# HGRN2 recurrence in four pairs of heads, its level updates on VectorE between the projections of the next pair

## The reference

```
q, z_fw, z_bw, i, g = split(h @ w_in, 5)          # each 512 x 1024, 8 heads of 128
log_f = log(lb + (1 - lb) * sigmoid(z));  k = 1 - exp(log_f)      # per direction
S_t = diag(f_t) S_{t-1} + k_t outer v_t ;  o_t = S_t^T silu(q_t)  # per head and direction
o = rmsnorm(o_fw + o_bw, out_norm) * silu(g);  return o @ w_o
```

## Time and profile before

| | us |
|---|---|
| median of 3 runs (lowest, highest) | 2341.68 (2337.03, 2342.49) |
| the profiled execution's own time | 2341.26 |
| its span, first to last instruction | 2339.5 |
| TensorE busy, share of the span | 2114.2, 90% |
| VectorE, ScalarE, GpSimd busy | 936.7, 614.8, 841.7 |
| mean granted clock | 0.939 |

### The profile page before, as it was taken

How to read it: one execution, slowest core, us unless ns; L and a number is a source line. 1 busy time by engine, 2 the same in 40 slices (tenths; PEclk the granted TensorE clock), 3 DMA queues, 4 the chain that set the end, 5 groups by cost and what they waited for, 6 DMA issues and landing times.

```text
span 2339.5 us, 31254 instructions
## 1 busy us (share of the span) xinstructions
PE 2114.2 (90%) x12424; PEld 1711.4 (73%) x12424; DVE 936.7 (40%) x1186; ACT 614.8 (26%) x789; POOL 841.7 (36%) x360
## 2 busy tenths in 40 slices
PE   7999999888999999999999977965997489999997
PEld 5888887644778888878888866754875477788885
DVE  4434414555273331145343123175318535543212
ACT  4222223233242222233222233210231023222221
POOL 2444442200224444424444442362246212444442
PEclk9999999899999999999999998976997589999998
DMA  3223332200223223322233321210121012332332
GB/s 137 95 94 99 92 97 80 63 18 1 74 71 99 90 98 92 99 79 91 98 98 92 93 85 54 85 44 1 55 82 48 1 37 80 91 99 90 94 99 76
DMA packets 51640, 179.68 MB, mean 77 GB/s; under 512 B 5728, under 2 KB 5856, under 8 KB 51552
## 3 DMA queue, kind: packets, MB, share of 16 engines
q1 hardware_dynamic: 51552, 178.40, 23.9%
HBM read 176.28 MB, written 2.10 MB: 76 GB/s over the span
## 4 chain that ended last, share of the span: by engine, by line
PE 73%; issue 13%; DVE 6%; POOL 6%; ACT 2%; DMA 1%; SPq 0%; POOLq 0%; DVEq 0%; ACTq 0%
PE psum L481 23%; PE psum L482 22%; PE psum L483 22%; POOL w_lo L403 3%; POOL k_lev L423 2%; PE psum L700 1%; DVE att L1263 1%; DVE prob L1275 1%; PE psum L693 1%; DVE q_lev L1334 0%; PE psum L761 0%; PE psum L573 0%; DVE xt L1101 0%; PE psum L819 0%; DVE t_a L1096 0%
## 5 line engine op out<-in xcount | busy, mean ns | idle before, releaser
L403 POOL TENSOR_TENSOR w_lo<-raw,w_hi 128x1024 fp32r<-128x1024 f32 (+1 forms) x324 | 766.5, 2366 | 1399.6 <-ACT w_hi L885 1399.6
L481 PE MATMUL psum<-xg_hi,w_hi 128*128 128x512 f32 x1832 | 730.7, 399 | 38.8 <-DMA const<-consts 15.8
L482 PE MATMUL psum<-xg_lo,w_hi 128*128 128x512 f32 x1832 | 722.5, 394 | 0.0
L483 PE MATMUL psum<-xg_hi,w_lo 128*128 128x512 f32 x1832 | 722.3, 394 | 0.0
L885 ACT ACTIVATE w_hi<-raw 128x1024 fp32r<-128x1024 f32 (+1 forms) x339 | 352.1, 1039 | 1046.3 <-DMA raw<-w_up 492.0
L481 PEld LDWEIGHTS psum<-xg_hi,w_hi 128*128 128x128 f32 x1832 | 348.7, 190 | 117.6 <-DMA const<-consts 15.8
L483 PEld LDWEIGHTS psum<-xg_hi,w_lo 128*128 128x128 f32 x1832 | 347.8, 190 | 80.1
L482 PEld LDWEIGHTS psum<-xg_lo,w_hi 128*128 128x128 f32 x1832 | 348.6, 190 | 74.7 <-issue 0.2
L481 PE MATMUL psum<-hid_hi,w_hi 128*128 128x512 f32 x704 | 273.9, 389 | 0.0
L483 PE MATMUL psum<-hid_hi,w_lo 128*128 128x512 f32 x704 | 273.9, 389 | 0.0
L482 PE MATMUL psum<-hid_lo,w_hi 128*128 128x512 f32 x704 | 273.9, 389 | 0.0
(11 more groups left out here) (162 smaller groups left out, 1499.2 us busy)
## 6 DMA issues: line engine op xcount, KB each, us to landing
raw<-w_up SPq DMA_DIRECT2D x176, 512.0 KB, 3.5
raw<-w_down SPq DMA_DIRECT2D x64, 512.0 KB, 3.6
raw<-w_hgrn SPq DMA_DIRECT2D x48, 512.0 KB, 3.5
raw<-w_down SPq DMA_DIRECT2D x32, 384.0 KB, 3.1
raw<-w_mla SPq DMA_DIRECT2D x19, 512.0 KB, 3.5
xt<-x_t SPq DMA_DIRECT2D x8, 256.0 KB, 6.4
out<-xt SPq DMA_DIRECT2D x8, 256.0 KB, 2.0
const<-consts SPq DMA_DIRECT2D x1, 305.0 KB, 8.0
```

The lines of the kernel that those rows point to most:

```text
L403: pool.tensor_tensor(w_lo[slot][:, 0:n], raw[slot][:, 0:n], w_hi[slot][:, 0:n].bitcast(F32), ALU.subtract).then_inc(w_ready, 1)
L481: first = pe.matmul(ps, w_hi[slot][:, at:at + n], hi, start=start, stop=False)
L482: pe.matmul(ps, w_hi[slot][:, at:at + n], lo, start=False, stop=False)
L483: return first, pe.matmul(ps, w_lo[slot][:, at:at + n], hi, start=False, stop=stop)
```

## The change

Four quarters of two heads (PAIR = 2) take the place of the two halves, and the code is written out instead of looped. `entry` and the two spare slots now serve HGRN2 too, so six groups run at its start. In a quarter, the 10 groups are: two for the values of this quarter, four for the gates and two for the queries of the next one, and two for the output gate of this one. One group stands ahead of each level unit. The last quarter has no next one; rounds of the output projection (`output_step`: one 128-feature block into four banks, 12 matmuls) stand between its levels instead.

Both directions of a level are one unit (`masked`, L771): 64 matmuls of 16 query columns, one mask and one `keep`. Queries of both directions come from one `q_raw`. Values are projected like all others and turned by four transposes (`turn_values`). The gates become `k_lev` and `gates` on ScalarE alone (`gate`, four activations). ScalarE takes the long-distance scores and the outputs out of PSUM. VectorE does both directions of the queries (L1531), the keys of both directions in one instruction (L1533), the gate products (L1536), and the low parts of the weights (`split`, L1341). GpSimd is left with the first tiles of HGRN2 and the last two.

```diff
-                    with loop(pool, 2, (hi, HGRN_HALF_TILES), (level, UNITS), (keys_ok, 2 * (N_UPDATES - 1)), stream=stream):
-                        hgrn_half()
-                    for _ in range(KB - ENTRY):
+                    for _ in range(PAIR):
+                        split()
+                    skip(HGRN_TILES - ENTRY - EXTRA - 2 * PAIR)
+                    for _ in range(PAIR):
                         split()
...
+            def update(n, m):          # VectorE
+                dve.wait_ge(level_ready, LEVELS_UP * n + m.bit_length())
+                for d in range(2):
+                    q = pairs(q_lev[n % 2], 1 - d, m)[:, :, 1 - d, :]
+                    dve.tensor_tensor(q, q, of_runs(n, d, d, m), ALU.mult)
+                k = crossed(k_lev[n % 2], m)
+                dve.tensor_tensor(k, k, crossed_runs(n, m), ALU.mult).then_inc(level_ready, 1)
+                if m < P:
+                    both = runs(n, m)[:, :, 0:N // m].rearrange("p d (b two) -> p d b two", two=2)
+                    dve.tensor_tensor(runs(n, 2 * m)[:, :, 0:N // m // 2], both[:, :, :, 0], both[:, :, :, 1],
+                                      ALU.mult).then_inc(dve_step, 1)
...
+                    keep(n, 1)
+                    update(n, 1)
+                    evict()
+                    split(s, t + 3)
+                    keep(n, 2)
+                    update(n, 2)
+                    evict()
+                    split(s, t + 4)
...
+                def gate(n, i):        # ScalarE
+                    z = next_temp()                         # waits for drained
+                    act.activation(t_c[:, :], z, ACT.Sigmoid).then_inc(act_step, 1)
+                    act.activation(keys, z, ACT.Sigmoid, scale=-1.0).then_inc(taken, 1)
+                    act.activation(keys, keys, ACT.Copy, scale=one_lb[:, d, head])
+                    act.activation(gates[n % 2][:, d, at], t_c[:, :], ACT.Identity, bias=lb[:, d, head],
+                                   scale=one_lb[:, d, head]).then_inc(gate_ready, 1)
...
+                    for i in range(Z_TILES):
+                        gate(n + 1, i)
+                        hi_part()
...
+                tail = TAIL_BANKS[0]   # TensorE
+                for n in range(QUARTERS):
+                    more = n + 1 < QUARTERS
+                    project(by_dve=n > 0)
+                    if n:
+                        o_statistics(n - 1, range(PAIR), tail)
+                    project(by_dve=n > 0)
+                    if n:
+                        pe.wait_ge(recip_made, recips.next())
+                        widen_o(n - 1, 0, tail)
+                    turn_values(n, 0)
+                    diagonal(n)
+                    project()
+                    if n:
+                        widen_o(n - 1, 1, tail)
+                    turn_values(n, 1)
+                    masked(n, 1)
+                    project()
+                    masked(n, 2, closing=not more)
+                    if not more:
+                        break
+                    project()
+                    masked(n, 4)
+                    project()
+                    masked(n, 8)
+                    project()
+                    masked(n, 16)
+                    project()
+                    within_64(n)
+                    project()
+                    within_128(n)
+                    project()
+                    within_256(n)
+                    for h in range(PAIR):
+                        across(n, h)
+                        values(n, h)
+                masked(n, 4)
+                output_step(0, tiles, banks)
+                masked(n, 8)
+                output_step(1, tiles, banks)
...
+                output_step(7, tiles, banks)
+                for _ in LATE:
+                    project()
+                for _ in range(PAIR):
+                    project(by_dve=False)
```

More of the change, by code:

```diff
@@ L53 @@
 MASKED = (1, 2, 4, 8, 16)
-N_MASKS = 1 + 2 * len(MASKED)
+N_MASKS = len(MASKED)
 GAIN_COL = 0
@@ L113, with tiles_freed_for @@
 TILE_SLOT = tile_slots()
+def tiles_freed_for(n):
+    earlier = [m for m in range(n) if TILE_SLOT[m] == TILE_SLOT[n]]
+    return earlier[-1] + 1 if earlier else None
 class Count:
@@ L838, in hgrn @@
-                    level_free.more += 4
-                    silu.more += HALF
-                    pe.wait_ge(o_squared, squares.next(HALF))
-                    for h in range(HALF):
-                        for b in range(TB):
-                            last = pe.matmul(psum[:, STAT, h * TB + b:h * TB + b + 1], o_sq[:, h, b * P:(b + 1) * P],
+                            last = pe.matmul(ps[:, b * P:(b + 1) * P], k_lev[n % 2][:, d, keys:keys + P],
+                                             q_lev[n % 2][:, 1 - d, queries:queries + P], start=True, stop=True)
@@ new lines, in within_256, with across @@
+                        last.then_inc(unit_done, 1)
+                def across(n, h):
+                    pe.wait_ge(level_ready, LEVELS_UP * n + 9)
+                    for j in range(2):
+                        ps = open_unit()
+                        for d in range(2):
+                            keys = h * SEQ + (d * 2 + j) * P
+                            queries = h * SEQ + (1 - d) * 2 * P
+                            last = pe.matmul(ps[:, (1 - d) * 2 * P:(2 - d) * 2 * P], k_lev[n % 2][:, d, keys:keys + P],
+                                             q_lev[n % 2][:, 1 - d, queries:queries + 2 * P], start=True, stop=True)
+                        last.then_inc(unit_done, 1)
@@ L1011, in hgrn @@
             def hgrn():
[L1012 to L1019 removed]
+                temps, units, steps, took, gated = Count(), Count(), Count(), Count(), Count()
@@ new lines, in query, with output_gate, unit @@
+                def query(j):
+                    z = next_temp()
+                    took.more += 1
+                    act.activation(q_raw[:, j * SEQ:(j + 1) * SEQ], z, ACT.Silu).then_inc(taken, 1)
+                def output_gate(n, j):
+                    z = next_temp()
+                    took.more += 1
+                    act.activation(y[:, n * PAIR + j, :], z, ACT.Silu).then_inc(taken, 1)
+                def unit():
+                    act.wait_ge(unit_done, units.next())
+                    return psum[:, UNIT_BANKS[(units.count - 1) % 2], :]
@@ new lines, in values_out, with nearest_out @@
+                def values_out(n, j):
+                    ps = unit().rearrange("p (b v) -> p b v", b=TB)
+                    act.activation(v_hgrn[n % 2][:, :, j * P:(j + 1) * P], ps, ACT.Copy).then_inc(unit_out, 1)
+                def nearest_out(n):
+                    act.wait_ge(score_out, SCORES * (n + 1))
+                    for g in range(P // SUB):
+                        rows = slice(g * SUB, (g + 1) * SUB)
+                        last = act.activation(near[rows, :, rows], nearest[rows, :, :], ACT.Copy)
+                    last.then_inc(near_made, 1)
@@ new lines, in o_hi @@
+                def o_hi(head):
+                    act.wait_ge(chunk_new, normed + head + 1)
+                    new.more += 1
+                    act.activation(xg_hi[:, head, :], y[:, head, :], ACT.Copy).then_inc(chunk_hi, 1)
+                hi_part()
+                gate(0, 0)
+                gate(0, 1)
+                hi_part()
+                gate(0, 2)
+                gate(0, 3)
+                hi_part()
+                query(0)
+                query(1)
+                for n in range(QUARTERS - 1):
+                    if n:
```

837 lines of the change are left out of this document (461 added, 376 removed).

## The result

The changed kernel takes 2232.6 us (median of 4 runs, 2231.0 to 2238.0) against 2340.6 us (4 runs, 2337.0 to 2342.5). The ratio is 0.9544, with a 95% interval of 0.9524 to 0.9565: 108 us less. The forecast was 2266 with a range from 2234 to 2308.

A forecast was written before the change was run, and what follows sets the result against it. A serial VectorE-ScalarE-VectorE chain was to set the pace: first A 1454.3, three quarters to 1765.4, last quarter to 1865.4, clock to 1870.4; 75.7 us saved, 2266 predicted, range 2234 to 2308.

The forecast's parts named there:

- first A: End of a quarter's first masked level unit; the first was forecast at 1454.3, with six groups done early.
- four gate steps: Level steps with a gate: serial chain VectorE, ScalarE, VectorE through the high part; 10.2, 9.6, 9.3, 9.2 us.
- from there to the last update's end: Query and output-gate steps, one activation each, 7.3, 6.6 and 6.6 us, then the last update, 2.65.
- scores and values: After a quarter's levels: heads of 10.6 and 6.35 us plus 0.5 waiting for ScalarE's copy and square; 17.5.
- head of the next quarter: Three groups 16.5, statistics 1.9, two widenings and two turnings 3.1, two small units 2.7; 24.2 us.
- last quarter with its 3 us of clock: VectorE's chain 50.5, scores, values and statistics 16.2, output rounds 8.5, groups 21.9: 97, plus 3 at 1.2 GHz; 100.
- clock in the steps: Level steps: waits of 2.3 us may halve TensorE's clock in the group behind; 5 us allowed in all.
- the entry: Start of HGRN2: six projection groups done by 1433.1 instead of 2.3; gain 3.7 groups, 20 us.
- 1 (TensorE's pace, 6.94 a step): Level steps: TensorE stays the bound; quarter 88 or so, about 42 us less, 2224; 10 in 100.
- 2: Level steps: clock drops in each and stays down for most of the group; 30 to 35 us more, 2298; 14 in 100.
- 4: Quarters: TensorE granted 1.2 GHz throughout, so slower than before; 150 us more, 2416; 3 in 100.
- 3: Levels: VectorE's crossed passes slower than plain ones or at the mean; 51 us more, 2317; 8 in 100.

The follow-up runs named there:

- Experiment 4: Changed kernel without the early start: TensorE waits for all eight input blocks, statistics and widening before the same six groups; 2260.6 us, ratio 0.9660.
- Experiment 1: Changed kernel with ScalarE's order turned: next weight tile's high part ahead of the gate or first query step in quarters 0 to 2; 2211.4 us, ratio 0.9447.
- 5: Changed kernel with VectorE taking the low part of the next weights one place later, behind the next level's updates; ScalarE's order unchanged; 2212.2 us, ratio 0.9458.
- experiment 7: Changed kernel with the six output steps among the last quarter's levels moved behind its values; 2257.6 us, ratio 0.9636.
- experiment 10: Changed kernel with the key products and the low weight parts both on GpSimd instead of VectorE; 2264.2 us, ratio 0.9683.
- experiment 8: Kernel before the change with only its levels' key products moved from GpSimd to VectorE; 2333.0 us, ratio 0.9971.

## Why the prediction was off

The mechanism was right and the sizes were too large. These are the terms of the sum, in us, against the changed kernel's trace (three numbers are the first three quarters):

| term | forecast | measured |
| --- | --- | --- |
| FFN end to first A | 65.9 | 65.0 |
| four gate steps | 38.3 | 37.1 |
| from there to the last update's end | 23.7 | 21.3, 21.3, 23.1 |
| scores and values | 17.5 | 15.5, 17.8, 15.3 |
| head of the next quarter | 24.2 | 22.9 |
| period of a quarter | 103.7 | 96.8, 99.1, 98.4 |
| last quarter with its 3 us of clock | 100 | 93.4 |
| clock in the steps | 5 | 0 |

The step that failed is "period 62 + 17.5 + 24.2 = 103.7": three periods were 311 and came out at 294.2, 16.9 less. Of these, 5.4 are the updates behind the gate steps, 3.9 the scores and values, 3.9 the head and 3.7 the gate steps. The last quarter gave 6.6, the clock allowance 5 and the entry 0.9: 29.4 together. The stretch began 1.7 us later in this execution, so it ended 27.7 us ahead of the 1870.4 of the prediction. The profiled execution took 2238.0, the slowest of its four; the median lies 5.4 below it, where I had taken the difference of the kernel before. The 1.4 us by which the median lies outside the range are less than these 5.4.

- **The entry: right, its worth undersized.** The first projection starts 7.4 us after the FFN's last matmul (7.7 forecast), the first A was within 1 us. Experiment 4 gives 24.7 us for the 20 of the prediction.
- **The gate steps: right.** 10.5, 9.1, 8.8 and 8.7 for 10.2, 9.6, 9.3 and 9.2, with VectorE's wait for the high part that was named as the sign (the terms of the sum add up to 8.91 and not 8.95, which changes nothing). Two errors nearly cancelled. The first key pass costs 2.21 us, not 1.23. On the other side I had added up durations, but an instruction starts before the one ahead of it has ended: 1.21 us for the two query passes, 1.14 for a key pass or a low part of 1.22 in a row.
- **TensorE's waits: wrong.** "It waits about 2.3 us in each" step, and 2 to 3 us ahead of each masked unit, was not seen. TensorE starts each quarter ahead of the chain, none of the units for distances 1 and 2 waits in the first three quarters, and over the whole stretch it waits for keys ahead of a masked unit five times, the longest in the last quarter:

```profile
engine line waited for: us in total, times, longest us
PE psum L771 <- DVE k_lev L1533: 10.6, 5, 4.7
```


- **The other updates: too long.** Query and output-gate steps took 6.6, 6.1 and 6.1 us where 7.3, 6.6 and 6.6 stood. It is the same overlap, without a slow pass to offset it. The last quarter's chain is the same term again, from the first mask to the end of its last update: 43.3 us where 50.5 stood. In the third quarter these updates took 23.1, because TensorE stood for 2.38 us inside the unit before them with no releaser in the trace, and VectorE then waited 1.7 us for TensorE's units. The prediction put such gaps at nothing with a group between; it had also placed the gap of 1.86 us in the earlier trace rows between two units, where the row shows it inside one (119 and 9 records).
- **Scores and values: too long.** I took the first head's 10.6 us from a place where half clock lasted for most of it. In the first quarter here only its first 3.68 us ran so, and the head took 8.1 us. In the second, half clock lasted nearly to its end and it took 10.4, near the 10.6 of the forecast. The windows of the second quarter's scores and values and of the head behind them show which of the two was longer:

```profile
1610.25:1628.05 17.80, 15.91 (x83) 13.70 (x84) 3.68 (x4) 4.28 (x8) 0.00 (x0) 0.74 0.00 1
1628.05:1650.94 22.89, 22.89 (x360) 19.46 (x359) 7.52 (x10) 7.27 (x10) 0.00 (x0) 1.00 0.22 70
```

- **The head of the next quarter: too long.** Its two widenings and two turnings took 1.9 us together where 3.1 stood.
- **The clock: right that it falls, wrong where it costs.** The group behind the wait of 1.96 us ran partly at 1.2 GHz, but the step is set by VectorE and ScalarE, and TensorE has 2 us of slack in it. A loss off the chain had been added to the chain. What it does cost, 2.3 us in the second quarter's scores and values, was in another term.
- **One mask, and fewer columns: right.** The mask of 256 columns takes 0.44 us (0.47 taken). The unit of 64 matmuls with 16 columns takes 1.40 to 1.43 us, not less than the 1.30 with 32 columns.
- **Rivals.** 1 (TensorE's pace, 6.94 a step) did not occur. What spoke against it was the order of the lists, and with another order (1 and 5) the steps are 7.06. Its price was wrong by its own numbers: a quarter of 88 in place of 103.7, three times, and 12 in the last are 59 us less, 2207, and not 42, 2224. Experiment 1 came to 2211 with quarters of about 89. The range began just above the 2224. 2 and 4 did not occur; experiment 7 shows something like 4 in the last quarter alone, where the filling is taken away. 3 occurred in one level of eight only, and for the keys alone. What the prediction said of GpSimd, that without its work a pass of 1024 columns is 1.23 us, held: the means are 1219 ns in the changed kernel and 1824 for 512 columns with all of that work back (experiment 10).
- **"The keys' weight now lies in VectorE's chain above"** was right but I saw no choice in it. The prediction had the chain in full and took the order for given, so it did not say what an exchange of two entries is worth: 21 us.

## What to carry to other kernels

Write down the lists of two engines that feed each other as one chain, and look for a short piece that the other engine waits for behind a long one that it doesn't: an exchange in either list gave 21 us here. Then add up the times from start to start, not durations, and add a loss only if it falls on the chain that sets the pace. Work that fills waits was free twice here, for its own time and for the clock that it held up, and moving work between VectorE and GpSimd has to be priced with what the one does to the other.

## What the hardware showed that I had not expected

- An elementwise pass whose pattern crosses two directions costs 2.21 us with runs of one element and 1.22 with all longer runs (1024 columns, fp32). Two passes with runs of one element that each stay in one direction (512 columns) cost 0.68 each.
- Beside a two-input pass on GpSimd, VectorE's own two-input passes stretch: 3.43 for 1.22 us, 5.15 for 1.29, a mean of 1824 for 688 ns. The first of these ends 1.08 us after GpSimd's pass (1466.79 and 1465.71), which is about what it takes by itself. The Trainium skill (GPSIMD Engine Reference, Key points) says that the two share SBUF interfaces when VectorE reads two SBUF inputs; the trace agrees, and these are its numbers here.
- Even so both engines together can be as fast as VectorE with both passes: 2.07 us for the query pass beside 2.42 for the key pass on GpSimd, against 2.5 one behind the other (experiment 8).
- ScalarE's activations with a bias or scale from a column take 0.72 to 0.80 us for 512 columns, the plain ones 0.63.
